# A hybrid decoder layer: three changes of order in the MLP's Strassen-like rounds, and a weight sum moved from GpSimd to VectorE

## The chip, the cores and the metric

The kernel runs on one core of a Trainium2 chip. The metric is the device time of one execution in microseconds (us), as the median of a few runs.

## What is computed

One decoder layer (DEPTH = 1) on 256 tokens of width 2048, everything in float32:

```
h = RMSNorm(x);  [b, c, xt, v] = h @ w_in            (2048 x 4096)
y_conv = b * causal_depthwise_conv3(c * xt)
y_pool = scale * per_group_linear(trailing_mean_w(v) - v)
x = x + concat(y_conv, y_pool) @ w_out               (2048 x 2048)
x = x + relu(RMSNorm(x) @ w_up)^2 @ w_down           (2048 x 8192, 8192 x 2048)
out = RMSNorm(x)
```

## The kernel before

**Precision.** TensorE multiplies in a reduced float32 format, so every operand is kept as a "hi" part and a "lo" part: ScalarE writes hi = round(raw), VectorE writes lo = raw - hi. A product is hi by hi, lo by hi and hi by lo. A weight is loaded into w_raw, split into w_hi (ScalarE, `hi_of`, L791) and w_lo (VectorE, `lo_of`, L1173), and used by TensorE. w_hi and w_lo have four slots each, used in turn, so hi of item g waits until TensorE has finished item g - 4 (`chunk_used`).

**Stages.** The projection w_in, the pool jobs, w_out, and then the MLP, which takes the span from about 290 us on. This case is about the MLP.

**The MLP.** w_up comes in 16 blocks t of 512 columns, each in four chunks of 1 MB. w_down is used in rounds d = t - 2: in round d (0 to 13) TensorE works on the four chunks of w_up block t = d + 2, and in between on w_down for blocks that are ready. Two blocks of hidden values with a half of w_down's columns form a 2 x 2 problem of quadrants that is done with seven products instead of eight. Each of the seven terms, one after another, is a product of a combination of value quadrants (S7, A11, N6, S5, A12, N3, A22) and a combination of weight quadrants (t3, b11, t2, t1, b21, t4, b22). An even and an odd round share the value combinations (slice s = d // 2).

**The order of TensorE in a round** (L587 to L608), written out by hand: up chunk 0, a11_b11, up chunk 1, n6_t2, a12_b21, up chunk 2, s7_t3 of round d + 1, s5_t1, up chunk 3, a22_t4, n3_b22. In round 0 s7_t3 of round 0 comes after up chunk 0. An up chunk is 16 hi matmuls (L557; the profile shows them at the helper's L395) and 16 lo matmuls (L398); a term is 8 matmuls with w_hi (L577, L579) and 4 with w_lo (L583). The same order of items (`item_order`, L38) numbers the weights for hi and lo.

**Folds.** Four terms go into bank NT of PSUM one after another, and VectorE adds or subtracts the bank into x after each (`fold`, L1203), with factors that make the accumulated sums come out right; a22_t4 goes on in the bank of s7_t3. TensorE waits for a fold before it writes on: a11_b11 for the fold of n3_b22 of round d - 1, n6_t2 for that of a11_b11, s5_t1 for that of n6_t2, n3_b22 for that of s5_t1. The folds count up one semaphore, and `fold_count` gives the count of each.

**Values.** When up chunk 3 of block t - 1 is done, ScalarE copies one half of the banks (`take_up`, L805), VectorE adds the other half and applies ReLU and the token's 1/rms (`add_up`, L1183, L1187), ScalarE squares (L810), VectorE makes the combinations ("parts", L1213, L1236, L1238, L1250), and both split them (`quad_hi` L816, `quad_lo` L1192).

**The weight sums of round d.** `sums[d % 2]` is loaded by SP with quadrant 1; GpSimd adds quadrant 3 by an accumulating DMA: that is t3 (`make_t3`, L371). After lo of s7_t3, and when quadrant 0 has landed in w_raw slot 2, the sum of both is t2 (L377 to L380): in the kernel before, a GpSimd addition over 128 x 2048. After lo of a11_b11 GpSimd adds quadrant 1 to slot 2 by DMA (t1), and after lo of n6_t2 it adds quadrant 2 to the sums (t4).

**VectorE's order in a round** (L1224 to L1279): fold s5_t1 (d - 1), lo up 0, add_up, lo a11_b11, parts, fold a22_t4 (d - 1), lo up 1, fold n3_b22 (d - 1), quad_lo's, lo n6_t2, quad_lo, lo a12_b21, fold a11_b11, quad_lo's, lo up 2, lo s7_t3 (d + 1), fold n6_t2, lo s5_t1, fold a12_b21, lo up 3, lo a22_t4, fold s7_t3 (d + 1), lo n3_b22. In even rounds there are two parts before the folds and one after, with two quad_lo's (L1192) more; in odd rounds one part before. In round 0 lo of s7_t3 stands after add_up.

After round 13 come eight plain products of w_down (`plain`, L621), the last of which wait for the last folds, and the final norm.

Of the kernel before, what the change touches and what calls it, by code (L numbers as in the profile page):

```python
# [15 lines left out]
NT = 4  # L16
# [7 lines left out]
FIRST_UP = FIRST_OUT + OUT_BLOCKS  # L24
UPS = D_FF // BLOCK_COLS
LEAD = 2
SEVENS = UPS - LEAD
# [25 lines left out]
ITEM = {name: FIRST_ITEM + i for i, name in enumerate(item_order())}  # L53
# [26 lines left out]
def build(nc, x_t, x_rows, w_stream, w_quads, pool_w, params, g_final, out):  # L80
# [4 lines left out]
    with ctx:  # L85
# [142 lines left out]
        def fold_count(d, term):  # L228

            if term == "s7_t3":  # L230
                return 1 if d == 0 else fold_count(d - 1, "a12_b21") + 1
            ahead = 1 if d + 1 < SEVENS else 0
            return 1 + 7 * d + {"a11_b11": 1, "n6_t2": 2, "a12_b21": 3, "s5_t1": 4 + ahead,
                                "a22_t4": 5 + ahead, "n3_b22": 6 + ahead}[term]

        def up_values(t):

# [7 lines left out]
        def bank_b(d):  # L245
            return NT + 1 + d % 2
# [112 lines left out]
        @block.gpsimd  # L359
        def _(pool):  # L360
            pool.memset(ones[:, :], 1.0).then_inc(consts_set, 1)
            pool.memset(win[:, :, :, 0:PAD], 0.0).then_inc(consts_set, 1)
            pool.wait_ge(x_lo_ready, KT)
            pool.memset(v[:, :, 0:PAD], 0.0).then_inc(v_pads_zero, 1)
            pool.wait_ge(pool_w_ready, 1)
            pool.memset(u[:, :, 0:2], 0.0).then_inc(u_pads_zero, 1)

            def add_quad(to, d, n, added):
                pool.dma_start(to, w_quads[4 * d + n, :, :], accum_op=ALU.add).then_inc(added, 16)  # L369

            def make_t3(d):  # L371
                pool.wait_ge(sum_base_loaded[d % 2], 16 * (d // 2 + 1))
                add_quad(sums[d % 2], d, 3, t3_added[d % 2])

            make_t3(0)
            for d in range(SEVENS):
                pool.wait_ge(lo_ready, ITEM["s7_t3", d] + 1)  # L377
                pool.wait_ge(raw_loaded[2], 16 * (FIRST_UP + LEAD + d + 1))
                pool.tensor_tensor(out=sums[d % 2], in0=sums[d % 2], in1=w_raw[:, 2, :], op=ALU.add)\  # L379
                    .then_inc(t2_added, 1)  # L380
                if d + 1 < SEVENS:
                    make_t3(d + 1)
                pool.wait_ge(t2_added, d + 1)
                pool.wait_ge(lo_ready, ITEM["a11_b11", d] + 1)
                add_quad(w_raw[:, 2, :], d, 1, t1_added)
                pool.wait_ge(lo_ready, ITEM["n6_t2", d] + 1)
                add_quad(sums[d % 2], d, 2, t4_added)
            pool.wait_ge(lo_ready, ITEM["a22_t4", SEVENS - 2] + 1)
            pool.dma_start(g_row, g_final[0:1, :].to_broadcast([P, D])).then_inc(g_loaded, 16)
# [256 lines left out]
        def _(act):  # L646
# [141 lines left out]
            def hi_of(g, raw):  # L788

                act.wait_ge(chunk_used, g - 3)  # L790
                act.activation(w_hi[:, g % 4, :], raw, ACT.Copy).then_inc(hi_ready, 1)  # L791
# [6 lines left out]
            def take_up(t):  # L798

                act.wait_ge(chunk_used, ITEM["up", t, CHUNKS - 1] + 1)  # L800
                if t >= 3:
                    act.wait_ge(quad_ready, quad_count((t - 3) // 2, N3))
                act.wait_ge(summed, turn(FIRST_UP) + t)
                banks = bank_halves(1 if t == 1 else 0, 1)
                act.activation(cross[:, :, :], banks, ACT.Copy).then_inc(cross_ready, 1)  # L805
# [23 lines left out]
            for t in range(LEAD, UPS):  # L829
                d, s = t - LEAD, (t - LEAD) // 2  # L830
                folding = d % 2 == 0
                up_hi(t, 0)
                take_up(t - 1)
                if d == 0:
                    act.wait_ge(t3_added[0], 16)
                    hi_of(ITEM["s7_t3", 0], sums[0])
                act.wait_ge(raw_loaded[2], 16 * (FIRST_UP + LEAD + d + 1))
                hi_of(ITEM["a11_b11", d], w_raw[:, 2, :])
                square_up(t - 1)
                up_hi(t, 1)  # L840
                if folding:
                    act.wait_ge(part_ready, parts + 2)
                    quad_hi(s, N6, part_1, "n6_t2")
                    quad_hi(s, S5, part_0, "s5_t1")
                elif s + 1 < SLICES - 1:
                    act.wait_ge(part_ready, parts + 1)
                    quad_hi(s + 1, S7, part_2, "s7_t3")
                else:
                    act.wait_ge(squared, t)
                    quad_hi(s + 1, A21, held[:, :, P:S])  # L850
                act.wait_ge(t2_added, d + 1)
                hi_of(ITEM["n6_t2", d], sums[d % 2])
                if folding:
                    act.wait_ge(squared, t)
                    quad_hi(s, A12, val[:, :, 0:P], "a12_b21")
                act.wait_ge(raw_loaded[3], 16 * (FIRST_UP + LEAD + 2 * d + 1))
                hi_of(ITEM["a12_b21", d], w_raw[:, 3, :])
                if folding:
                    act.wait_ge(part_ready, parts + 3)
                    quad_hi(s, N3, part_1, "n3_b22")  # L860
                    quad_hi(s, A22, val[:, :, P:S], "a22_t4")
                else:
                    act.wait_ge(squared, t)
                    quad_hi(s + 1, A11, held[:, :, 0:P], "a11_b11")
                parts += 3 if folding else 1
                up_hi(t, 2)
                if d + 1 < SEVENS:
                    act.wait_ge(t3_added[(d + 1) % 2], 16 * ((d + 1) // 2 + 1))
                    hi_of(ITEM["s7_t3", d + 1], sums[(d + 1) % 2])
                act.wait_ge(t1_added, 16 * (d + 1))  # L870
                hi_of(ITEM["s5_t1", d], w_raw[:, 2, :])
                up_hi(t, 3)
                act.wait_ge(t4_added, 16 * (d + 1))
                hi_of(ITEM["a22_t4", d], sums[d % 2])
                act.wait_ge(raw_loaded[3], 16 * (FIRST_UP + LEAD + 2 * d + 2))
                hi_of(ITEM["n3_b22", d], w_raw[:, 3, :])
# [31 lines left out]
        def _(dve):  # L908
# [262 lines left out]
            def lo_of(g, raw):  # L1171
                dve.wait_ge(hi_ready, g + 1)
                dve.tensor_tensor(out=w_lo[:, g % 4, :], in0=raw, in1=w_hi[:, g % 4, :].bitcast(F32),  # L1173
                                  op=ALU.subtract).then_inc(lo_ready, 1)
# [4 lines left out]
            def add_up(t):  # L1179

                to = up_values(t)
                dve.wait_ge(cross_ready, IN_CROSSES + t + 1)
                dve.tensor_tensor(out=to[:, :, :], in0=bank_halves(1 if t == 1 else 0, 0),  # L1183
                                  in1=cross[:, :, :], op=ALU.add).then_inc(summed, 1)
                dve.wait_ge(summed, turn(FIRST_UP) + t + 1)
                dve.wait_ge(inv_rms_ready, 2)
                dve.scalar_tensor_tensor(out=to[:, :, :], in0=to[:, :, :], scalar=0.0, in1=by_token(),  # L1187
                                         op0=ALU.max, op1=ALU.mult).then_inc(value_ready, 1)
# [7 lines left out]
            def fold(term, d, bank, t, n, op):  # L1196

                dve.wait_ge(chunk_used, ITEM[term, d] + 1)
                count = fold_count(d, term)
                if count > 1:  # L1200
                    dve.wait_ge(folded, count - 1)
                to = x_quad(d, t, n)
                dve.tensor_tensor(out=to, in0=to, in1=ps[:, bank, :], op=op).then_inc(folded, 1)  # L1203
# [20 lines left out]
            for t in range(LEAD, UPS):  # L1224
# [2 lines left out]
                if d:  # L1227
                    fold("s5_t1", d - 1, NT, 1, 1, ALU.subtract)
                up_lo(t, 0)
                add_up(t - 1)  # L1230
                if d == 0:
                    lo_of(ITEM["s7_t3", 0], sums[0])
                lo_of(ITEM["a11_b11", d], w_raw[:, 2, :])
                dve.wait_ge(squared, t)
                if folding:
# [4 lines left out]
                elif s + 1 < SLICES - 1:  # L1240
                    make_s7()
                if d:
                    fold("a22_t4", d - 1, bank_b(d - 1), 1, 0, ALU.add)
                up_lo(t, 1)
                if d:
                    fold("n3_b22", d - 1, NT, 0, 1, ALU.subtract)
                if folding:
                    quad_lo(s, N6, part_1)
                    quad_lo(s, S5, part_0)
# [31 lines left out]
            def plain_lo(f):  # L1281
                lo_of(ITEM["plain", f], w_raw[:, plain_raw(f)[0], :])
# [8 lines left out]
            fold("s5_t1", SEVENS - 1, NT, 1, 1, ALU.subtract)  # L1291
            plain_lo(0)
            add_up(UPS - 1)
            plain_lo(1)
            fold("a22_t4", SEVENS - 1, bank_b(SEVENS - 1), 1, 0, ALU.add)
            dve.wait_ge(squared, UPS)
            quad_lo(last_slice, A12, val[:, :, 0:P])
            quad_lo(last_slice, A22, val[:, :, P:S])
# [86 lines left out]
```

## Time and profile before

| what | value |
|---|---|
| median of 3 runs | 990.32 us (989.34 to 990.75) |
| the profiled execution, its own time | 989.43 us |
| its span, first to last instruction | 987.6 us |
| mean granted TensorE clock | 0.994 of full speed |
| TensorE busy | 954.1 us (97%) |
| VectorE busy | 787.4 us (80%) |
| ScalarE busy | 526.7 us (53%) |
| GpSimd busy | 114.8 us (12%) |
| mean DMA rate | 241 GB/s |

Times in the rows are microseconds from the first instruction; where one row stands for several instructions (x16), its time is that from the start of the first to the end of the last. PE is TensorE's matmuls, PEld its weight loads, DVE is VectorE, ACT ScalarE, POOL GpSimd. In square brackets stands how long the engine was idle before the instruction and what ended that. The ends of matmuls are modelled, and they overlap: the start of the next one is the better mark.

### The profile page before, as it was taken

The page shows a single profiled execution, that of the slowest core. Times are in us where ns is not written, and L with a number is a line of the kernel's source. Part 1 is how long each engine was busy: PE and PEld are TensorE (multiplying, and loading weights), DVE is VectorE, ACT ScalarE, POOL GpSimd, SP SyncE. Part 2 cuts the span into 40 slices and gives each one's busy share as a digit, 9 for nine tenths or more (in the row PEclk, how much of TensorE's full clock was granted, in tenths as well). Part 3 has the DMA queues.
Part 4 walks back from the last instruction along what each step waited for, and adds up shares of the span by engine and source line. Part 5 has one row for each costly group of instructions (what it writes and reads, how often), then busy time and mean ns, then how long its engine had stood idle before and what let it go on. Part 6 is the DMA issues. An engine that isn't in the chain of part 4 may idle for free.

```text
span 987.6 us, 12019 instructions
## 1 busy us (share of the span) xinstructions
PE 954.1 (97%) x4920; PEld 817.1 (83%) x4920; DVE 787.4 (80%) x605; ACT 526.7 (53%) x420; POOL 114.8 (12%) x65
## 2 busy tenths in 40 slices
PE   8999999999999969999999999999999999999996
PEld 7888888888888858888888888888888888888885
DVE  6597677655554789798988979989998997998864
ACT  6644435444543456565665556556555655646642
POOL 0000000000000303202031220203212020220000
PEclk9999999999999989999999999999999999999999
DMA  9956552644558198897989889898798979878822
GB/s 341 388 192 235 177 206 105 230 177 171 188 196 291 57 295 248 303 250 261 305 263 284 257 259 275 255 329 236 261 263 276 299 241 322 226 247 223 314 101 86
DMA packets 35763, 237.85 MB, mean 241 GB/s; under 512 B 3968, under 2 KB 4224, under 8 KB 7808
## 3 DMA queue, kind: packets, MB, share of 16 engines
q1 hardware_dynamic: 29232, 190.85, 50.3%
q0 software_dynamic: 6192, 45.09, 23.6%
q10 hardware_dynamic: 288, 1.18, 0.3%
q8 instruction: 37, 0.61, 0.2%
q14 instruction: 14, 0.11, 0.0%
HBM read 235.01 MB, written 2.10 MB: 240 GB/s over the span
## 4 chain that ended last, share of the span: by engine, by line
PE 62%; issue 16%; DVE 13%; ACT 6%; DMA 2%; SPq 0%; ACTq 0%; DVEq 0%
PE ps L395 22%; PE ps L398 12%; PE ps L486 9%; ACT w_hi L791 5%; PE ps L577 5%; PE ps L621 4%; PE ps L579 4%; PE ps L583 4%; DVE w_lo L1173 3%; DVE x L1203 3%; DMA w_raw<-w_stream 2%; DVE cross L1236 1%; DVE win L1187 1%; DVE val L1187 1%; DVE val L1183 1%
## 5 line engine op out<-in xcount | busy, mean ns | idle before, releaser
L395 PE MATMUL ps<-act_a,w_hi 128*128 128x512 f32 x1472 | 349.7, 390 | 0.0
L1173 DVE TENSOR_TENSOR w_lo<-w_raw,w_hi 128x2048 fp32r<-128x2048 f32 x120 | 316.7, 2639 | 10.2 <-ACT w_hi L791 9.0
L395 PEld LDWEIGHTS ps<-act_a,w_hi 128*128 128x128 f32 x1472 | 274.2, 188 | 55.5
L791 ACT ACTIVATE w_hi<-w_raw 128x2048 fp32r<-128x2048 f32 x120 | 229.5, 1913 | 71.0 <-PE ps L583 48.9
L398 PEld LDWEIGHTS ps<-act_a,w_lo 128*128 128x128 f32 x1472 | 188.5, 191 | 8.8 <-DVE w_lo L1173 1.9
L398 PE MATMUL ps<-act_a,w_lo 128*128 128x256 f32 x1472 | 191.2, 283 | 1.4 <-DVE w_lo L1173 1.4
L577 PE MATMUL ps<-w_hi,act_b 128*128 128x512 f32 x392 | 155.6, 397 | 18.8 <-DVE x L1203 18.8
L912 DVE TENSOR_TENSOR w_lo<-w_raw,w_hi 128x2048 fp32r<-128x2048 f32 x52 | 118.5, 2290 | 68.4 <-ACT w_hi L654 67.7
L579 PE MATMUL ps<-w_hi,act_b 128*128 128x512 f32 x392 | 154.1, 393 | 0.0
L1173 DVE TENSOR_TENSOR w_lo<-mix_mem,w_hi 128x2048 fp32r<-128x2048 f32 x42 | 104.8, 2496 | 48.6 <-ACT w_hi L791 48.1
L654 ACT ACTIVATE w_hi<-w_raw 128x2048 fp32r<-128x2048 f32 x52 | 98.9, 1911 | 65.5 <-PE ps L398 39.0
L791 ACT ACTIVATE w_hi<-mix_mem 128x2048 fp32r<-128x2048 f32 x42 | 80.2, 1910 | 89.4 <-PE ps L398 87.4
L379 POOL TENSOR_TENSOR mix_mem<-mix_mem,w_raw 128x2048 f32<-128x2048 f32 x14 | 76.9, 5494 | 265.2 <-DMA w_raw<-w_quads 233.9
L583 PE MATMUL ps<-w_lo,act_b 128*128 128x512 f32 x392 | 104.9, 389 | 0.0
L577 PEld LDWEIGHTS ps<-w_hi,act_b 128*128 128x128 f32 x392 | 74.3, 189 | 35.4 <-DVE x L1203 21.6
L583 PEld LDWEIGHTS ps<-w_lo,act_b 128*128 128x128 f32 x392 | 73.6, 188 | 15.5
L579 PEld LDWEIGHTS ps<-w_hi,act_b 128*128 128x128 f32 x392 | 74.4, 190 | 14.1
L1203 DVE TENSOR_TENSOR x<-x,ps 128x512 f32<-128x512 f32 x98 | 66.7, 681 | 3.3 <-PE ps L583 2.7
L486 PE MATMUL ps<-w_hi,act_b 128*128 128x512 f32 x256 | 68.8, 390 | 0.0
L369 POOL DMA_DIRECT2D mix_mem<-w_quads x28 | 24.5, 874 | 368.5 <-DMA mix_mem<-w_quads 272.2
L486 PEld LDWEIGHTS ps<-w_hi,act_b 128*128 128x128 f32 x256 | 47.8, 188 | 9.7
L805 ACT ACTIVATE cross<-ps 128x1024 f32<-128x1024 f32 x16 | 16.4, 1025 | 56.4 <-PE ps L398 56.4
(103 smaller groups left out, 593.6 us busy)
## 6 DMA issues: line engine op xcount, KB each, us to landing
w_raw<-w_stream SPq DMA_DIRECT2D x108, 1024.0 KB, 6.6
w_raw<-w_quads SPq DMA_DIRECT2D x50, 1024.0 KB, 8.6
mix_mem<-w_quads POOLq DMA_DIRECT2D x28, 1024.0 KB, 10.1
mix_mem<-w_quads SPq DMA_DIRECT2D x14, 1024.0 KB, 4.7
w_raw<-w_quads POOLq DMA_DIRECT2D x14, 1024.0 KB, 10.8
w_raw<-w_stream SPq DMA_DIRECT2D x16, 256.0 KB, 7.6
x<-x_rows SPq DMA_DIRECT2D x2, 1024.0 KB, 17.5
mix_mem<-x_t SPq DMA_DIRECT2D x3, 512.0 KB, 7.9
```

The lines of the kernel that those rows point to most:

```text
L379: pool.tensor_tensor(out=sums[d % 2], in0=sums[d % 2], in1=w_raw[:, 2, :], op=ALU.add)\
L395: return pe.matmul(ps[:, bank, :], weights_hi, act, start=first, stop=False)
L398: return pe.matmul(ps[:, bank, 0:S], weights_lo, act[:, 0:S], start=False, stop=last)
L486: mm = pe.matmul(ps[:, NT * parity + t, :], a[:, at:at + P], cols, start=first and i == 0, stop=last and i == 2)
L577: pe.matmul(to, quads[:, quad, k, 0:P], weights_of(w_hi, g, k), start=first and k == 0, stop=False, skip_group_check=not first)
L579: pe.matmul(to, quads[:, quad, k, P:2 * P], weights_of(w_hi, g, k), start=False, stop=False, skip_group_check=not first)
L583: mm = pe.matmul(to, quads[:, quad, k, 0:P], weights_of(w_lo, g, k), start=False, stop=k == CK - 1, skip_group_check=not first)
L654: act.activation(w_hi[:, c, :], w_raw[:, c, :], ACT.Copy).then_inc(hi_ready, 1)
L791: act.activation(w_hi[:, g % 4, :], raw, ACT.Copy).then_inc(hi_ready, 1)
L912: dve.tensor_tensor(out=w_lo[:, c, :], in0=w_raw[:, c, :], in1=w_hi[:, c, :].bitcast(F32), op=ALU.subtract)\
L1173: dve.tensor_tensor(out=w_lo[:, g % 4, :], in0=raw, in1=w_hi[:, g % 4, :].bitcast(F32), op=ALU.subtract).then_inc(lo_ready, 1)
L1203: dve.tensor_tensor(out=to, in0=to, in1=ps[:, bank, :], op=op).then_inc(folded, 1)
```

## The change

Four things are changed:

- The sum t2 (L379) is made by VectorE, between add_up and lo of a11_b11, with the same waits. GpSimd keeps only its DMAs.
- In a round, VectorE folds n3_b22 (d - 1) before lo up 1 and a22_t4 (d - 1) after it; before, it was the other way round. `fold_count` follows.
- In round 0, hi and lo of s7_t3 come before take_up and add_up instead of after them.
- After the last round, the fold of a22_t4 comes before the lo of plain product 1 instead of after it.

```diff
--- before.py
+++ after.py
@@ -229,9 +229,11 @@
 
             if term == "s7_t3":
                 return 1 if d == 0 else fold_count(d - 1, "a12_b21") + 1
-            ahead = 1 if d + 1 < SEVENS else 0
-            return 1 + 7 * d + {"a11_b11": 1, "n6_t2": 2, "a12_b21": 3, "s5_t1": 4 + ahead,
-                                "a22_t4": 5 + ahead, "n3_b22": 6 + ahead}[term]
+            if d + 1 < SEVENS:
+                ends = {"s5_t1": 5, "n3_b22": 6, "a22_t4": 7}
+            else:
+                ends = {"s5_t1": 4, "a22_t4": 5, "n3_b22": 6}
+            return 1 + 7 * d + ({"a11_b11": 1, "n6_t2": 2, "a12_b21": 3} | ends)[term]
 
         def up_values(t):
 
@@ -374,13 +376,8 @@
 
             make_t3(0)
             for d in range(SEVENS):
-                pool.wait_ge(lo_ready, ITEM["s7_t3", d] + 1)
-                pool.wait_ge(raw_loaded[2], 16 * (FIRST_UP + LEAD + d + 1))
-                pool.tensor_tensor(out=sums[d % 2], in0=sums[d % 2], in1=w_raw[:, 2, :], op=ALU.add)\
-                    .then_inc(t2_added, 1)
                 if d + 1 < SEVENS:
                     make_t3(d + 1)
-                pool.wait_ge(t2_added, d + 1)
                 pool.wait_ge(lo_ready, ITEM["a11_b11", d] + 1)
                 add_quad(w_raw[:, 2, :], d, 1, t1_added)
                 pool.wait_ge(lo_ready, ITEM["n6_t2", d] + 1)
@@ -830,10 +827,10 @@
                 d, s = t - LEAD, (t - LEAD) // 2
                 folding = d % 2 == 0
                 up_hi(t, 0)
-                take_up(t - 1)
                 if d == 0:
                     act.wait_ge(t3_added[0], 16)
                     hi_of(ITEM["s7_t3", 0], sums[0])
+                take_up(t - 1)
                 act.wait_ge(raw_loaded[2], 16 * (FIRST_UP + LEAD + d + 1))
                 hi_of(ITEM["a11_b11", d], w_raw[:, 2, :])
                 square_up(t - 1)
@@ -1227,9 +1224,13 @@
                 if d:
                     fold("s5_t1", d - 1, NT, 1, 1, ALU.subtract)
                 up_lo(t, 0)
-                add_up(t - 1)
                 if d == 0:
                     lo_of(ITEM["s7_t3", 0], sums[0])
+                add_up(t - 1)
+                dve.wait_ge(lo_ready, ITEM["s7_t3", d] + 1)
+                dve.wait_ge(raw_loaded[2], 16 * (FIRST_UP + LEAD + d + 1))
+                dve.tensor_tensor(out=sums[d % 2], in0=sums[d % 2], in1=w_raw[:, 2, :], op=ALU.add)\
+                   .then_inc(t2_added, 1)
                 lo_of(ITEM["a11_b11", d], w_raw[:, 2, :])
                 dve.wait_ge(squared, t)
                 if folding:
@@ -1240,10 +1241,10 @@
                 elif s + 1 < SLICES - 1:
                     make_s7()
                 if d:
-                    fold("a22_t4", d - 1, bank_b(d - 1), 1, 0, ALU.add)
+                    fold("n3_b22", d - 1, NT, 0, 1, ALU.subtract)
                 up_lo(t, 1)
                 if d:
-                    fold("n3_b22", d - 1, NT, 0, 1, ALU.subtract)
+                    fold("a22_t4", d - 1, bank_b(d - 1), 1, 0, ALU.add)
                 if folding:
                     quad_lo(s, N6, part_1)
                     quad_lo(s, S5, part_0)
@@ -1291,8 +1292,8 @@
             fold("s5_t1", SEVENS - 1, NT, 1, 1, ALU.subtract)
             plain_lo(0)
             add_up(UPS - 1)
+            fold("a22_t4", SEVENS - 1, bank_b(SEVENS - 1), 1, 0, ALU.add)
             plain_lo(1)
-            fold("a22_t4", SEVENS - 1, bank_b(SEVENS - 1), 1, 0, ALU.add)
             dve.wait_ge(squared, UPS)
             quad_lo(last_slice, A12, val[:, :, 0:P])
             quad_lo(last_slice, A22, val[:, :, P:S])
```

## Rows read from the trace of the kernel before

**Rows 1.** The page's engines: busy us (share of the span) and instructions.
```profile
PE 954.1 (97%) x4920; PEld 817.1 (83%) x4920; DVE 787.4 (80%) x605; ACT 526.7 (53%) x420; POOL 114.8 (12%) x65
```
**Rows 2.** Waits: engine, line, releaser: us in total, times, longest us.
```profile
PE ps L577 <- DVE x L1203: 18.8, 14, 6.5
```
**Rows 3.** TensorE's timeline, an odd and an even round: start us, us, instruction.
```profile
557.96 2.07 PE L398 MATMUL ps<-act_a,w_lo 128*128 128x256 f32 x16
560.57 0.50 PE L577 MATMUL ps<-w_hi,act_b 128*128 128x512 f32 x1 [0.54 <-DVE x L1203]
...
563.43 3.79 PE L395 MATMUL ps<-act_a,w_hi 128*128 128x512 f32 x16
...
568.97 0.40 PE L577 MATMUL ps<-w_hi,act_b 128*128 128x512 f32 x1
...
571.72 0.39 PE L577 MATMUL ps<-w_hi,act_b 128*128 128x512 f32 x1
...
603.41 0.50 PE L577 MATMUL ps<-w_hi,act_b 128*128 128x512 f32 x1 [1.26 <-DVE x L1203]
...
611.82 0.40 PE L577 MATMUL ps<-w_hi,act_b 128*128 128x512 f32 x1
```
**Rows 4.** The page's groups: busy us, mean ns of one | idle before, releaser.
```profile
L791 ACT ACTIVATE w_hi<-mix_mem 128x2048 fp32r<-128x2048 f32 x42 | 80.2, 1910 | 89.4 <-PE ps L398 87.4
L379 POOL TENSOR_TENSOR mix_mem<-mix_mem,w_raw 128x2048 f32<-128x2048 f32 x14 | 76.9, 5494 | 265.2 <-DMA w_raw<-w_quads 233.9
```
**Rows 5.** VectorE's timeline, from the odd round into the even one.
```profile
565.56 0.68 DVE L1203 TENSOR_TENSOR x<-x,ps 128x512 f32<-128x512 f32 x1
...
585.00 6.11 DVE L1173 TENSOR_TENSOR w_lo<-w_raw,w_hi 128x2048 fp32r<-128x2048 f32 x1
...
593.83 1.21 DVE L1183 TENSOR_TENSOR val<-ps,cross 128x1024 f32<-128x1024 f32 x1
...
596.22 2.28 DVE L1173 TENSOR_TENSOR w_lo<-w_raw,w_hi 128x2048 fp32r<-128x2048 f32 x1
598.42 0.68 DVE L1236 TENSOR_TENSOR cross<-val,win 128x512 f32<-128x512 f32 x1
...
599.87 0.69 DVE L1203 TENSOR_TENSOR x<-x,ps 128x512 f32<-128x512 f32 x1
...
610.59 0.68 DVE L1203 TENSOR_TENSOR x<-x,ps 128x512 f32<-128x512 f32 x1
```
**Rows 6.** The timeline of all engines around 590 us: GpSimd's sum and ScalarE's copy.
```profile
583.29 5.66 POOL L379 TENSOR_TENSOR mix_mem<-mix_mem,w_raw 128x2048 f32<-128x2048 f32 x1 [18.70 <-DMA w_raw<-w_quads]
...
591.19 1.03 ACT L805 ACTIVATE cross<-ps 128x1024 f32<-128x1024 f32 x1 [3.56 <-PE ps L398]
```
**Rows 7.** The page's DMA issues: count, KB each, median us to landing.
```profile
w_raw<-w_quads POOLq DMA_DIRECT2D x14, 1024.0 KB, 10.8
```
**Rows 8.** Timelines of ScalarE, VectorE and TensorE in the first round.
```profile
330.57 1.03 ACT L805 ACTIVATE cross<-ps 128x1024 f32<-128x1024 f32 x1 [6.52 <-PE ps L398]
...
338.43 5.10 DVE L1236 TENSOR_TENSOR cross<-val,win 128x512 f32<-128x512 f32 x1
...
353.81 1.47 DVE L1203 TENSOR_TENSOR x<-x,ps 128x512 f32<-128x512 f32 x2
...
355.33 0.80 PE L577 MATMUL ps<-w_hi,act_b 128*128 128x512 f32 x1 [6.52 <-DVE x L1203]
...
362.36 3.79 PE L395 MATMUL ps<-act_a,w_hi 128*128 128x512 f32 x16
```
**Rows 9.** A window: us, busy us of each engine, TensorE clock, DMA share, GB/s.
```profile
352.00:353.00 1.00, 0.00 (x0) 0.00 (x0) 1.00 (x1) 1.00 (x2) 0.11 (x1) 0.50 1.04 246
```
**Rows 10.** Timelines of VectorE and TensorE at the start of the plain products.
```profile
932.76 2.29 DVE L1173 TENSOR_TENSOR w_lo<-w_raw,w_hi 128x2048 fp32r<-128x2048 f32 x1
934.96 0.68 DVE L1203 TENSOR_TENSOR x<-x,ps 128x512 f32<-128x512 f32 x1
...
935.75 1.17 PE L621 MATMUL ps<-w_hi,act_b 128*128 128x512 f32 x4 [1.02 <-issue]
```

## The prediction, made before the change was run

> **What bounds the kernel now.** I read the page's table of engines first: TensorE is busy 97% of the span [rows 1]. So only time in which TensorE stands still can be won. The table of waits shows where that is: matmuls of L577, the first product of a term of w_down, waited 14 times for the fold at L1203, 18.8 us in all [rows 2]. The timeline of TensorE sorts these 14. One, in the first round (d = 0), is 6.52 us [rows 8]. The other 13 add to 12.28 us and recur with the parity of d, always before a11_b11, which needs the fold of n3_b22 of the round before: 1.26 us in the six even rounds (603.41 stands for them), 0.54 us in five of the seven odd ones (560.57), 4.72 us in the seven together [rows 3]. A last gap of 1.02 us stands before the plain products [rows 10].
>
> A stall costs more than its idle time. A w_up chunk without one takes 568.97 - 563.43 = 5.54 us, and the lo half that ends it started at 557.96; the next start without a stall comes 1.91 us after it (my reading of the same rows: the 16 lo products step by 0.12), so at 559.87, and it came at 560.57: 0.70. The term then took 563.43 - 560.57 = 2.86 us against 571.72 - 568.97 = 2.75 [rows 3]. So each stall costs its idle time plus 0.27 us: 1.53 us in an even round.
>
> Next, who is late. VectorE runs the even round without a gap from 585.00 on [rows 5]. One instruction there, a w_lo subtraction, took 6.11 us where its neighbours step by 2.20 us (596.22 to 598.42). GpSimd's sum ran from 583.29 to 588.95, over its start [rows 6]. Such a long VectorE instruction stands beside each of the 14 sums; in the first round it is the 5.10 us at 338.43, where its kind takes 0.68 us elsewhere [rows 5, 8]. The sum itself has a mean of 5.49 us on GpSimd [rows 4].
>
> **The change part by part.**
>
> *The sum leaves GpSimd.* The long instruction falls from 6.11 to 2.28 us, 3.83 us less. VectorE would then be free for add_up at 593.83 - 3.83 = 590.00, but ScalarE's copy of the cross half starts at 591.19, when TensorE has ended the chunk, and takes 1.03 us [rows 6]. So add_up starts at 592.25, not 593.83: only 1.58 us of the 3.83 is of use, 2.25 us is slack.
>
> *The sum goes to VectorE.* No row has an f32 addition of 128x2048 there. From below it is bounded by the subtraction of the same size, which also reads two SBUF operands and steps by 2.20 us [rows 5]; from above by the sum on GpSimd, 5.49 us [rows 4]. I take 2.20, since engine, shape and operand kinds are those of the subtraction. At 5.49 the first and the six even rounds would lose 3.3 us each and the seven odd ones about 2.1, together 38 us; no VectorE row is near that, so the range leaves it out. The Trainium skill (GPSIMD Engine Reference, Key points) says that VectorE is structurally about twice as fast for elementwise work: by that factor 5.49 us would become 2.75, and the time would be 3.8 us longer than forecast below (seven chains by 0.55). The subtraction's row, 2.4 times faster than the GpSimd sum, goes before it.
> The sum stands between add_up and the lo of a11_b11. Its new waits end long before: its w_raw slot had landed when GpSimd's sum began at 583.29, 11 us earlier. Queued behind it are the lo of a11_b11, the two parts, both folds, the lo of a12_b21 and the fold of a11_b11. All of them come -1.58 + 2.20 = 0.62 us later than now.
>
> *n3_b22 is folded ahead of a22_t4 and of a w_up lo.* It takes the place at 599.87 [rows 5]: start 600.49, end 601.17. TensorE wants it when the chunk ends, at 603.41 - 1.42 = 601.99. The stall before a11_b11 is gone in the even rounds; in the odd ones, with one part less to make, there is more room still.
> What is late next is the fold of a11_b11, for which n6_t2 waits. Even round: it starts at 610.59 now [rows 5], so at 611.21, and ends at 611.89. TensorE would be there at 611.82 - 1.53 = 610.29 [rows 3]. New stall: n6_t2 starts at 611.95, 1.66 us late, 1.77 with the slow start. Six even rounds: 6 x (1.53 - 1.77) = **-1.4 us**, a loss. Odd round: the fold starts at 565.56 + 0.62 and ends at 566.9, and TensorE wants it at 568.97 - 0.81 = 568.16 [rows 3, 5]. No stall, so the whole 4.72 + 7 x 0.27 = **+6.6 us** is won.
> The later fold of a22_t4 costs nothing: TensorE's next use of its bank is s7_t3, a whole w_up chunk after n6_t2, which waits for more. If that cover were gone, the price would be the 2.8 us that it moves.
>
> *First round.* The s7_t3 pair moves ahead of take_up and add_up. ScalarE idles 6.52 us before that take_up [rows 8], which covers the pair: a hi of 1.91 us [rows 4] and, behind it, the lo of 2.2 us. Its t3 is made by the first DMA that GpSimd issues in this stage. The lo of s7_t3 thus leaves the chain and the sum enters it, 2.20 against 2.20. The instruction at 338.43 loses 5.10 - 0.68 = 4.42 us. Every instruction from there to the pair of folds at 353.81 follows without a gap, so they end at 350.9 and n6_t2 starts there instead of at 355.33: **+4.4 us**. TensorE has stood still since 355.33 - 6.52 = 348.8 in the trace; its wait for a w_up lo in the chunk before, whose lo comes 4.4 us sooner too, goes as well, so it will stand from about 347, and a gap of 4 us stays.
> The clock: in that standstill it fell to half (1.2 of 2.4 GHz), as granted at 352 to 353 [rows 9]; the two terms after it took 362.36 - 355.33 = 7.03 us instead of 2.86 + 2.75 = 5.61 [rows 8]. With the shorter gap this 1.4 us may be lost as before or won whole. Between a standstill of 6.5 us that loses the clock and stalls of 1.3 us that keep it there is no row for 4 us; I take the middle, **+0.7 us**, and keep 0 and 1.4 for the range.
>
> *Tail.* The fold of a22_t4 moves ahead of plain_lo(1), to 932.76, and ends at 933.44 instead of 935.64. TensorE's last term ends about 934.7, so the gap of 1.02 us goes, with the slow start **+1.2 us** [rows 10]. plain_lo(1) comes 0.6 us later, at 935.6 done; its product starts 5.4 us after the first, at about 940.
>
> *GpSimd's queue.* Its three accumulating DMAs a round stay. t3 no longer stands behind the sum, so it is issued up to 0.5 us sooner, in the first round much sooner. t1 and t4 follow the lo of a11_b11 and n6_t2, so they come 0.6 us later. They land in 10.8 us [rows 7], and their readers on TensorE, s5_t1 and a22_t4, stand two chunks and three or four terms on, at least 2 x 5.54 + 3 x 2.75 = 19 us. SP's loads wait for the same lo's and shift by as little. Cost nothing; without that slack 0.6 us a round.
>
> Sum: 4.4 + 0.7 + 6.6 - 1.4 + 1.2 = 11.5 us. The profiled execution took 989.43 us (span 987.6), which gives 977.9; the median of the runs, 990.32, is 0.9 above it, so I forecast **978.8 us**.
>
> **The rivals.**
> 1. *The long VectorE instruction has another cause than the sum* (the DMAs around it, say). Then the 3.83 us stays and 2.20 us is added. Against the forecast the first round loses 4.4 + 0.7, the six even rounds 6 x 1.58 = 9.5, and the odd ones get a stall of 568.50 - 568.16 and a slow start, 0.45 x 7 = 3.2: 17.8 us, so 978.8 + 17.8 = 996.6, **slower than before**. It decides from about 3.5 us of the 3.83 staying. Against it: all 14 coincide, also where the sum lay over another instruction. The Trainium skill (SBUF — State Buffer, SBUF: two separate sides) says that a VectorE instruction with two SBUF inputs and a GpSimd one that reads SBUF exclude each other for the whole instruction; by that rule the long instruction goes with the sum, and the trace agrees: 588.95 - 585.00 = 3.95 us of overlap, 3.83 us longer. Chance 0.04.
> 2. *The sum costs more on VectorE than the subtraction*, by 0.5 to 1 us (two waits ahead of it, in-place output). Each 0.1 us costs 0.7 us (six even chains and the first); at +0.5 it gives 982.3. The odd rounds stay out up to +1.2. Every two-input SBUF row of VectorE speaks against it. Chance 0.10.
> 3. *The first round's gain does not come*: DMA is busy in full there, and an earlier round may meet loads that have not landed. Then 978.8 + 5.1 = 983.9. For it: a DMA share of 1.04 at 352 to 353 [rows 9]. Against: no wait for a load there now, and t3's transfer leaves that stretch. Chance 0.10.
> 4. *The n6_t2 stall is smaller* because something in the chain has slack I don't see; without it 978.8 - 6 x 1.77 = 968. Against: VectorE's rows have no gap in that chain. Chance 0.06.
>
> **How the numbers follow.** Forecast with its bounds (clock 0.7 either way, spread of runs 0.7): 977 to 980.5, chance 0.70. The range reaches to rivals 2 and 3 above and partly towards 4: 975 to 984. A measurement of this kernel can tell about 0.2% (2 us). Faster by more than that: forecast and rivals 2 to 4, 0.95. Slower: rival 1 nearly, 0.03. Within: 0.02, the edge of rival 1 where part of the slowdown stays.
>
> **What would show it.** No GpSimd TENSOR_TENSOR and no VectorE instruction over 2.4 us among the w_lo ones; 14 new ones of 2.28 us. In the waits, L577 waits for L1203 seven times instead of 14: about 4 us at d = 0, and about 1.5 us before n6_t2 at each even d; none in odd rounds. A pair of rounds gets 0.81 - 0.24 = 0.6 us shorter. No gap before the plain products. Stalls before a11_b11 that stay, or waits of ScalarE for a DMA, would make it wrong.

## The result, and the profile after

The changed kernel takes **979.29 us** (median of 4 runs, 978.88 to 979.58), the kernel before 990.54 beside it: ratio 0.9885 (95% interval 0.9868 to 0.9902), 11.3 us faster. 978.8 was forecast.

The span went from 987.6 to 977.8 us. The page of the changed kernel, its engines and the groups that answer to [rows 1, 4]; in the changed kernel the subtraction is L1170 (was L1173), the sum L1232, the fold L1200 (was L1203):

```profile
PE 951.9 (97%) x4920; PEld 816.8 (84%) x4920; DVE 763.8 (78%) x619; ACT 527.0 (54%) x420; POOL 37.8 (4%) x51
...
L1170 DVE TENSOR_TENSOR w_lo<-w_raw,w_hi 128x2048 fp32r<-128x2048 f32 x120 | 274.3, 2286 | 9.2 <-ACT w_hi L788 8.2
```

And from its table of groups for VectorE:

```profile
L1232 DVE TENSOR_TENSOR mix_mem<-mix_mem,w_raw 128x2048 f32<-128x2048 f32 x14 | 32.0, 2285 | 0.0
```

VectorE has 14 instructions more and is busy 23.6 us less: the 14 sums add 32.0 us, and what GpSimd's sums had stretched is gone (the w_lo subtractions of L1170 have means of 2286 and, from the sums, 2291 ns, and the longest takes 2.30 us). The waits of TensorE for a fold, which answer to [rows 2]:

```profile
PE ps L574 <- DVE x L1200: 12.9, 7, 3.8
```

Seven instead of 14. TensorE's timeline shows which (columns as in [rows 3]): the one of round 0, and the even rounds, all before n6_t2; 606.45 stands for six of 1.50 to 1.51 us.

```profile
350.82 0.80 PE L574 MATMUL ps<-w_hi,act_b 128*128 128x512 f32 x1 [3.81 <-DVE x L1200]
...
602.87 2.07 PE L395 MATMUL ps<-act_a,w_lo 128*128 128x256 f32 x16
606.45 0.50 PE L574 MATMUL ps<-w_hi,act_b 128*128 128x512 f32 x1 [1.51 <-DVE x L1200]
```

VectorE's timeline of that even round, from add_up to the fold of a11_b11 (answers to [rows 5]), with ScalarE's copy ahead of it from the timeline of ScalarE:

```profile
585.69 1.03 ACT L802 ACTIVATE cross<-ps 128x1024 f32<-128x1024 f32 x1 [3.56 <-PE ps L395]
```

```profile
586.75 1.23 DVE L1180 TENSOR_TENSOR val<-ps,cross 128x1024 f32<-128x1024 f32 x1 [2.17 <-ACT cross L802]
...
589.15 2.29 DVE L1232 TENSOR_TENSOR mix_mem<-mix_mem,w_raw 128x2048 f32<-128x2048 f32 x1
591.35 2.28 DVE L1170 TENSOR_TENSOR w_lo<-w_raw,w_hi 128x2048 fp32r<-128x2048 f32 x1
...
605.71 0.68 DVE L1200 TENSOR_TENSOR x<-x,ps 128x512 f32<-128x512 f32 x1
```

VectorE now waits 2.17 us for ScalarE's copy before add_up (2.25 were reckoned); the sum steps by 2.20 us; the fold of a11_b11 ends at 606.39, and TensorE goes on at 606.45. From the copy's start to the end of this fold it is 606.39 - 585.69 = 20.70 us now and was 611.27 - 591.19 = 20.08 [rows 5, 6]: the chain is the 0.62 us longer that were worked out. To n6_t2 it is 20.76 us now and was 20.63 [rows 3, 6], because TensorE, held up before a11_b11, came after that fold then and waits for it now.

Round 0 and the clock, in windows of the changed kernel (columns as in [rows 9]):

```profile
348.00:349.00 1.00, 0.00 (x0) 0.00 (x0) 1.00 (x1) 1.00 (x1) 0.00 (x0) 1.00 1.34 279
349.00:350.00 1.00, 0.00 (x0) 0.00 (x0) 0.97 (x2) 0.69 (x1) 0.00 (x0) 0.66 0.70 123
...
354.00:355.00 1.00, 1.00 (x4) 0.81 (x3) 1.00 (x2) 0.00 (x0) 0.00 (x0) 0.50 0.90 344
```

The granted clock fell to half in the 3.8 us standstill too, and in this execution it came back later than before: in TensorE's timeline the chunk after the two terms starts at 358.85, so they took 358.85 - 350.82 = 8.03 us, against 7.03 [rows 8]. That 1.0 us is not the length of the standstill. Two of the runs below that keep this part of the changed kernel have the same standstill, and there the two terms took 7.13 and 6.94 us (this is the run with the fold order undone):

```profile
351.31 0.80 PE L572 MATMUL ps<-w_hi,act_b 128*128 128x512 f32 x1 [3.83 <-DVE x L1198]
...
358.25 3.79 PE L390 MATMUL ps<-act_a,w_hi 128*128 128x512 f32 x16
```

And after a standstill of 6.52 us, as before the change, they took 8.16 us in the run with the folds alone. So the clock's cost varies between 1.3 and 2.6 us over the 5.6 us of the full clock, after the short and after the long standstill alike.

The tail: VectorE folds at 924.05, TensorE goes from its last term to the plain products without a gap ([rows 10] had one of 1.02 us).

```profile
924.05 0.68 DVE L1200 TENSOR_TENSOR x<-x,ps 128x512 f32<-128x512 f32 x1
```

```profile
924.96 1.07 PE L580 MATMUL ps<-w_lo,act_b 128*128 128x512 f32 x4
925.86 1.07 PE L618 MATMUL ps<-w_hi,act_b 128*128 128x512 f32 x4
```

### The profile page after: what moved, and what is told of

Its sections match the earlier page's. It is cut to its first block, busy times and chain, and to the rows that moved or that the text cites. A ratio compares the mean times of both kernels' runs of the same rounds, so it can differ in the third digit from the quotient of the medians.

```text
span 977.8 us, 12003 instructions
## 1 busy us (share of the span) xinstructions
PE 951.9 (97%) x4920; PEld 816.8 (84%) x4920; DVE 763.8 (78%) x619; ACT 527.0 (54%) x420; POOL 37.8 (4%) x51
## 4 chain that ended last, share of the span: by engine, by line
PE 79%; DVE 10%; issue 5%; DMA 2%; ACT 2%; SPq 1%; ACTq 0%; DVEq 0%
PE ps L392 28%; PE ps L395 15%; PE ps L483 9%; PE ps L574 8%; PE ps L576 7%; PE ps L580 7%; PE ps L618 4%; DMA w_raw<-w_stream 2%; DVE w_lo L1170 2%; DVE mix_mem L1232 2%; DVE act_b L1189 1%; DVE x L1200 1%; DVE val L1180 1%; ACT cross L802 1%; DVE cross L1239 1%
## 5 line engine op out<-in xcount | busy, mean ns | idle before, releaser
L1170 DVE TENSOR_TENSOR w_lo<-w_raw,w_hi 128x2048 fp32r<-128x2048 f32 x120 | 274.3, 2286 | 9.2 <-ACT w_hi L788 8.2
L909 DVE TENSOR_TENSOR w_lo<-w_raw,w_hi 128x2048 fp32r<-128x2048 f32 x52 | 118.5, 2291 | 67.3 <-ACT w_hi L651 66.6
L1170 DVE TENSOR_TENSOR w_lo<-mix_mem,w_hi 128x2048 fp32r<-128x2048 f32 x42 | 96.2, 2291 | 38.2 <-ACT w_hi L788 37.7
L580 PE MATMUL ps<-w_lo,act_b 128*128 128x512 f32 x392 | 105.6, 391 | 0.0
L580 PEld LDWEIGHTS ps<-w_lo,act_b 128*128 128x128 f32 x392 | 74.2, 189 | 15.6
L1200 DVE TENSOR_TENSOR x<-x,ps 128x512 f32<-128x512 f32 x98 | 66.8, 681 | 2.6 <-PE ps L580 2.0
L483 PE MATMUL ps<-w_lo,act_b 128*128 128x512 f32 x128 | 39.4, 389 | 0.0
## 6 DMA issues: line engine op xcount, KB each, us to landing
mix_mem<-w_quads POOLq DMA_DIRECT2D x28, 1024.0 KB, 10.8
x<-x_rows SPq DMA_DIRECT2D x2, 1024.0 KB, 16.2
```

Source lines behind the costliest of these rows:

```text
L483: mm = pe.matmul(ps[:, NT * parity + t, :], a[:, at:at + P], cols, start=first and i == 0, stop=last and i == 2)
L580: mm = pe.matmul(to, quads[:, quad, k, 0:P], weights_of(w_lo, g, k), start=False, stop=k == CK - 1, skip_group_check=not first)
L909: dve.tensor_tensor(out=w_lo[:, c, :], in0=w_raw[:, c, :], in1=w_hi[:, c, :].bitcast(F32), op=ALU.subtract)\
```

## The experiments

The theory, called C: TensorE is let go by VectorE's folds, so only what moves along the chain from ScalarE's copy to the fold that TensorE needs counts. Its rival, called G: GpSimd's sum, which held VectorE up for 3.83 us a round, was the loss, and the orders are trimmings. The sum of the parts came out right, but the prediction had never said which part won, the move or the orders. All medians are set beside 990.3 to 990.9 us for the kernel before and 979.3 us for the changed one.

**The move of the sum alone** (the kernel before, with this):

```diff
-                pool.wait_ge(lo_ready, ITEM["s7_t3", d] + 1)
-                pool.wait_ge(raw_loaded[2], 16 * (FIRST_UP + LEAD + d + 1))
-                pool.tensor_tensor(out=sums[d % 2], in0=sums[d % 2], in1=w_raw[:, 2, :], op=ALU.add)\
-                    .then_inc(t2_added, 1)
...
-                pool.wait_ge(t2_added, d + 1)
...
+                dve.wait_ge(lo_ready, ITEM["s7_t3", d] + 1)
+                dve.wait_ge(raw_loaded[2], 16 * (FIRST_UP + LEAD + d + 1))
+                dve.tensor_tensor(out=sums[d % 2], in0=sums[d % 2], in1=w_raw[:, 2, :], op=ALU.add)\
+                   .then_inc(t2_added, 1)
                 lo_of(ITEM["a11_b11", d], w_raw[:, 2, :])
```

> The sum on VectorE, every order as before. Theory C (the chain: what counts is when VectorE's folds let TensorE go on): in a steady round VectorE reaches add_up 1.58 us sooner but carries 2.20 us more, so n3_b22 is folded 0.62 us later and both kinds of stall before a11_b11 grow: 13 x 0.62 = +8.1 us; the first round wins 4.42 - 2.20 = 2.2. In all 990.5 + 5.9, about 996 us, slower than before. Theory G (GpSimd's sum was the loss, the orders are trimmings): most of the 11 us gain is here, 980 to 984 us.

Measured: 999.29 us (ratio to before 1.0098, 1.0078 to 1.0118), **9 us slower than before**. G falls: the change's headline, alone, makes the kernel slower. The even stalls before a11_b11 have grown by 0.63 us each, and four of the seven odd ones by 0.62, as C has it (timeline of TensorE; 1.26 and 0.54 in [rows 3]):

```profile
518.23 0.50 PE L572 MATMUL ps<-w_hi,act_b 128*128 128x512 f32 x1 [1.89 <-DVE x L1198]
...
562.60 0.50 PE L572 MATMUL ps<-w_hi,act_b 128*128 128x512 f32 x1 [1.16 <-DVE x L1198]
```

C's figure is 3 us short. The windows of this run show why: behind the stall of 1.89 us the clock fell to half for about 3 us.

```profile
518.20:519.00 0.80, 0.77 (x3) 0.67 (x4) 0.77 (x2) 0.80 (x1) 0.00 (x0) 1.00 1.03 215
519.00:519.50 0.50, 0.50 (x4) 0.38 (x3) 0.50 (x1) 0.50 (x1) 0.00 (x0) 1.00 1.02 213
519.50:520.00 0.50, 0.50 (x3) 0.40 (x2) 0.47 (x2) 0.46 (x1) 0.00 (x0) 0.59 1.10 229
...
522.50:523.00 0.50, 0.50 (x3) 0.41 (x2) 0.50 (x2) 0.32 (x1) 0.15 (x1) 0.50 1.04 442
523.00:524.00 1.00, 1.00 (x6) 0.83 (x5) 0.97 (x2) 1.00 (x1) 0.72 (x1) 1.00 0.32 131
```

From this round's a11_b11 to the next one's is 562.60 - 518.23 = 44.37 us, where a pair with the clock kept takes 42.75 (432.00 to 474.75): 1.6 us. It happened in three of the six even rounds, 4.9 us. That is more than the missing 3 us, because the other three odd stalls hardly grew: the seven went from 4.72 to 7.39 us together, 1.7 us less than C has it.

**The folds alone** (the kernel before; VectorE's order and `fold_count` as in the change):

```diff
                 if d:
-                    fold("a22_t4", d - 1, bank_b(d - 1), 1, 0, ALU.add)
+                    fold("n3_b22", d - 1, NT, 0, 1, ALU.subtract)
                 up_lo(t, 1)
                 if d:
-                    fold("n3_b22", d - 1, NT, 0, 1, ALU.subtract)
+                    fold("a22_t4", d - 1, bank_b(d - 1), 1, 0, ALU.add)
```

> Only the folds of n3_b22 and a22_t4 change places; the sum stays on GpSimd, round 0 and the tail stay. Theory C: the stall before a11_b11 goes in all 13 rounds (the seven odd ones win 6.6 us); in the six even ones n6_t2 waits instead, 1.15 us against 1.53: +2.3. About 8.9 us faster than before, 981.6 us. Theory G: little, 988 to 990.5 us.

Measured: 981.93 us (0.9912, 0.9895 to 0.9928), as C has it. No stall in odd rounds; six of 0.88 us before n6_t2.

**All of the orders without the move** (the changed kernel, with the first diff of this section backwards):

> The changed kernel with the sum back on GpSimd (all of the orders, not the move). Theory C: the stall before n6_t2 in the six even rounds is 0.62 us shorter than with the sum on VectorE, 3.7 us in all; round 0 is the same within 1 us, because GpSimd's sum now begins while VectorE still waits for ScalarE's copy. About 975.5 us (974.5 to 977), faster than the changed kernel. Theory G: the gain is mostly lost, 985 to 989 us.

Measured: 971.87 us (0.9812, 0.9795 to 0.9828), **7.4 us faster than the changed kernel**. The even stall is 0.88 us instead of 1.51, six times 0.63. In round 0 the gap is 1.96 us instead of 3.81, and the clock stayed full behind it, which C's figure had left out and which puts the result below its range: 1.9 us of gap and 1.3 to 2.4 of clock. So the long instruction of round 0 goes by the order alone, and the sum on VectorE takes 1.9 us of that back. The timeline of TensorE in this run:

```profile
351.55 0.50 PE L579 MATMUL ps<-w_hi,act_b 128*128 128x512 f32 x1 [1.96 <-DVE x L1205]
435.33 0.50 PE L579 MATMUL ps<-w_hi,act_b 128*128 128x512 f32 x1 [0.88 <-DVE x L1205]
```

**The fold order undone** (the changed kernel, the diff of the second experiment backwards):

> The changed kernel with the folds of n3_b22 and a22_t4 in their old places (the sum on VectorE, round 0 and tail as changed). Theory C: all 13 rounds stall before a11_b11 as in the run with the sum alone, 2.15 us in the even rounds and 1.43 in the odd ones, against 1.77 and 0: +2.3 and +10.0 us, and the stalls near 1.9 us cost the clock in about half of the even rounds, 1.6 us each: 979.3 + 12.3 + 4.8 = 996 us (992 if the clock holds). Theory G: 981 us or less.

Measured: 994.93 us (1.0044, 1.0026 to 1.0062). With the sum on VectorE this one exchange is worth 15.6 us; even stalls are 1.89 us, odd ones 1.16, and the clock fell behind three of the six.

**GpSimd's sum and the VectorE instruction at once** (the changed kernel; VectorE's instruction leaves the values as they are):

```diff
+                pool.wait_ge(lo_ready, ITEM["s7_t3", d] + 1)
+                pool.wait_ge(raw_loaded[2], 16 * (FIRST_UP + LEAD + d + 1))
+                pool.tensor_tensor(out=sums[d % 2], in0=sums[d % 2], in1=w_raw[:, 2, :], op=ALU.add)\
+                    .then_inc(t2_by_pool, 1)
...
-                dve.tensor_tensor(out=sums[d % 2], in0=sums[d % 2], in1=w_raw[:, 2, :], op=ALU.add)\
+                dve.wait_ge(t2_by_pool, d + 1)
+                dve.tensor_tensor(out=sums[d % 2], in0=sums[d % 2], in1=sums[d % 2], op=ALU.max)\
```

> The changed kernel, but GpSimd makes the sum where it did before, and VectorE an instruction of the same size in place of its sum (a maximum with itself). Both costs at once, the price of rival 1 of the prediction. If GpSimd's sum is what holds VectorE up: 14 long VectorE instructions are back, 1.58 us of each is on the chain, even rounds lose 6 x 1.58, odd ones 7 x 0.45, round 0 up to 1.5: 979.3 + 13.5 = about 993 us. If something else held it up in the kernel before, no long instruction comes back and the time is 979 to 980 us.

Measured: 994.81 us (1.0044, 1.0031 to 1.0057). The long instruction is back with GpSimd's sum in 13 of the 14 rounds (in round 0 the sum lies over add_up, see the last section), in one round as 6.12 us from 586.32, beside GpSimd's 5.57 us from 584.73 (timelines of VectorE and GpSimd):

```profile
586.32 6.12 DVE L1175 TENSOR_TENSOR w_lo<-w_raw,w_hi 128x2048 fp32r<-128x2048 f32 x1
```

```profile
584.73 5.57 POOL L382 TENSOR_TENSOR mix_mem<-mix_mem,w_raw 128x2048 f32<-128x2048 f32 x1 [16.25 <-DMA w_raw<-w_quads]
```

So the sum on GpSimd is the cause of the long instruction, which was only argued before, and another cause, as rival 1 has it, is out. The price of having both, 15.5 us, is near the 17.8 of rival 1 and the 13.5 above, but in part by luck, since the places are others: even rounds stall twice, 0.66 to 1.00 us before a11_b11 and 2.1 us before n6_t2, and odd rounds not at all. The clock fell in three of the six, 4.8 us, which more than makes up for the 3.2 us of the odd rounds.

**A longer chain** (the changed kernel, one more VectorE instruction behind the sum; values stay):

```diff
+                dve.wait_ge(t2_once, d + 1)
+                half_sum = sums[d % 2][:, 0:CHUNK_W // 2]
+                dve.tensor_tensor(out=half_sum, in0=half_sum, in1=half_sum, op=ALU.max)\
+                   .then_inc(t2_added, 1)
```

> The changed kernel with a second VectorE instruction right behind the sum, over half its columns (the maximum of each element with itself, so values stay), about 1.15 us and a wait of 0.1 us. Theory C with the chain as worked out: each of the six even rounds and round 0 lose all of it, 7 x 1.25 = 8.8 us, the odd rounds nothing, because their fold of a11_b11 is 1.26 us early: 988 us. If VectorE's sum were a matter of its load and not of the chain, all 14 rounds would lose alike (17.5 us, 997 us), or none (979 us) while it has idle time.

Measured: 990.88 us (1.0005, 0.9995 to 1.0015), no faster than the kernel before. Odd rounds lose nothing, even ones 0.35 us before a11_b11 and 0.65 more before n6_t2, and a slow start each:

```profile
515.50 0.50 PE L575 MATMUL ps<-w_hi,act_b 128*128 128x512 f32 x1 [0.35 <-DVE x L1201]
526.20 0.50 PE L575 MATMUL ps<-w_hi,act_b 128*128 128x512 f32 x1 [2.15 <-DVE x L1201]
```

So the chain has the length that was worked out. The 2.8 us over C's figure are again the clock, lost behind two of the six stalls of 2.15 us.

**Round 0 and the tail, each undone** (the changed kernel with the order of before at the one place):

```diff
                 up_hi(t, 0)
+                take_up(t - 1)
                 if d == 0:
                     act.wait_ge(t3_added[0], 16)
                     hi_of(ITEM["s7_t3", 0], sums[0])
-                take_up(t - 1)
...
-                if d == 0:
-                    lo_of(ITEM["s7_t3", 0], sums[0])
                 add_up(t - 1)
+                if d == 0:
+                    lo_of(ITEM["s7_t3", 0], sums[0])
```

> The changed kernel with the s7_t3 pair of round 0 behind take_up and add_up again. Theory C: the lo stands in the chain, n6_t2 of round 0 starts 2.2 us later, and the clock is lost either way: 981.5 us. Rival: the pair had cover there too, 979.3 us.

Measured: 981.33 us (0.9902, 0.9887 to 0.9918), 2.0 more. n6_t2 of round 0 starts at 353.00 instead of 350.82.

```diff
-            fold("a22_t4", SEVENS - 1, bank_b(SEVENS - 1), 1, 0, ALU.add)
             plain_lo(1)
+            fold("a22_t4", SEVENS - 1, bank_b(SEVENS - 1), 1, 0, ALU.add)
```

> The changed kernel with the last fold of a22_t4 behind plain_lo(1) again. Theory C: the gap of 1.02 us before the plain products is back with its slow start, 979.3 + 1.2 = 980.5 us. Rival: the products behind it have slack and give it back by the end, 979.3 us.

Measured: 980.55 us (0.9900, 0.9883 to 0.9917), 1.3 more, and the gap of 1.02 us is back. Both differences are near what the runs can tell; the timelines carry them.

**The next stall taken away** (the changed kernel):

```diff
                 lo_of(ITEM["n6_t2", d], sums[d % 2])
-                if folding:
-                    quad_lo(s, A12, val[:, :, 0:P])
-                lo_of(ITEM["a12_b21", d], w_raw[:, 3, :])
                 if d == 0:
                     fold("s7_t3", 0, bank_b(0), 1, 1, ALU.subtract)
                 fold("a11_b11", d, NT, 0, 0, ALU.add)
+                if folding:
+                    quad_lo(s, A12, val[:, :, 0:P])
+                lo_of(ITEM["a12_b21", d], w_raw[:, 3, :])
```

> The changed kernel, and in each round the fold of a11_b11 stands ahead of the lo of a12_b21 (in round 0 that of s7_t3 with it), 2.2 to 2.9 us sooner. Theory C: no stall before n6_t2 in even rounds, 6 x 1.77 = 10.6 us; in round 0 2.9 us less, and TensorE then stands for 1 us only, so the clock is kept and 2.4 us more are won: 963.4 us (965.8 if the clock falls all the same). Rival D (VectorE as a whole is the bound of an even round, so the wait only moves on to the next fold, before s5_t1): half or less of the 10.6 us, 969 us or more.

Measured: **963.09 us** (0.9725, 0.9708 to 0.9741), 16.2 us below the changed kernel. One stall is left in the whole of the rounds, and from 352 to 940 us TensorE is busy without a gap (window: us, then PE, PEld, DVE, ACT, POOL busy, clock, DMA share, GB/s):

```profile
347.77 0.50 PE L574 MATMUL ps<-w_hi,act_b 128*128 128x512 f32 x1 [0.90 <-DVE x L1200]
```

```profile
352.00:940.00 588.00, 588.00 (x2998) 503.71 (x2996) 517.17 (x365) 346.12 (x236) 33.44 (x39) 1.00 0.89 271
```

VectorE, 88% busy there, was never the bound as a whole: rival D falls.

**The same with the sum on GpSimd** (both edits together):

> The kernel with the fold of a11_b11 ahead of the lo of a12_b21, and the sum on GpSimd again. Theory C: with that fold early nothing waits for VectorE in a steady round, so where the sum is made does not matter: 962 to 963.5 us, as with the sum on VectorE (963.1), perhaps 0.9 us less in round 0. If the move of the sum is worth something by itself it shows here, 966 us or more.

Measured: **961.86 us** (0.9705, 0.9692 to 0.9718), the fastest here. In this run GpSimd still holds VectorE up in every round but the first, and it costs nothing (groups of VectorE; 2286 ns in the changed kernel):

```profile
L1175 DVE TENSOR_TENSOR w_lo<-w_raw,w_hi 128x2048 fp32r<-128x2048 f32 x120 | 323.9, 2699 | 8.9 <-ACT w_hi L793 7.7
```

The 1.2 us that it is faster than the run before are near what the runs can tell; the 0.90 us of idle time and the slow start of round 0, which are gone, are of that size.

## Why the prediction was right, step by step

- *The long instruction goes with the sum, of 3.83 us only 1.58 of use.* Right: add_up waits 2.17 us for ScalarE, and the run with both instructions shows the cause.
- *2.20 us on VectorE.* Right: 2.285 us each, steps of 2.20. The factor of two of the Trainium skill (GPSIMD Engine Reference, Key points) would have given 2.75; the measurement decides for the subtraction's row.
- *Odd rounds +6.6 us.* Right: no stall in any.
- *Even rounds -1.4 us.* Right: six of 1.51 us idle before n6_t2, where 1.66 less the 0.16 of modelled overlap were forecast.
- *Round 0 +4.4 us.* Right in size: n6_t2 at 350.82 instead of 355.33. But the orders alone give more, counted from the start of a11_b11: 13.12 us to n6_t2, against 14.98 in the changed kernel and 19.40 before.
- *The clock +0.7 us.* Wrong, the one mis-sized term: a standstill of 3.8 us lost the clock as one of 6.5 did. In the two profiled executions the term is **-1.0** (8.03 against 7.03 us), but over the kept traces the two terms took 8.03, 7.13 and 6.94 us after 3.8 us and 7.03 and 8.16 after 6.5, so what the change does to it is about 0, and the rest is chance. The range for this term, 0 to 1.4, should have reached below zero, as it left out that this loss varies from one execution to the next.
- *Tail +1.2 us.* Right: 1.3 by its undoing.
- *Sum.* The terms give 11.5; the profiled executions differ by 989.43 - 979.58 = 9.85. The 1.7 us between are the clock's term in these two. With 0 for it the terms give 10.8, near the 11.3 by which the median fell. Part of the closeness of 978.8 to 979.29 is luck all the same: the median before lies 1.1 us above its profiled run, the median after 0.3 below.
- *Rivals.* 1: the sum was the cause, so its condition was not met; its price was about right. 2 and 3 did not come. 4 neither: the stall before n6_t2 is there in full.

What the prediction left unsaid stands in its own numbers: -1.58 + 2.20 is a loss of 0.62 us a round. The move costs, and the orders win:

| the sum on | order before | orders of the change | and the fold of a11_b11 early |
|---|---|---|---|
| GpSimd | 990.3 | 971.9 | 961.9 |
| VectorE | 999.3 | 979.3 | 963.1 |

## What to carry to other kernels

An instruction that another engine stretches costs only what the stretch puts on the chain after its slack; read what stands behind it (here a wait for ScalarE of 2.25 us) before paying 2.2 us to remove 3.8. When several edits come together, price each of them by itself: the headline edit can be the one that loses. Where one engine's order sets another free, put what the other waits for ahead of what it needs only later: moving one fold past one or two subtractions was worth 16 us here, twice, with the sum on VectorE (with it on GpSimd the first of the two was worth 8.4, the second 10.0).

## What was not expected of the hardware

- **Short stalls can cost the clock.** Of the even-round stalls of 1.5 us in the changed kernel none was followed by a fall; of those of 1.89 us in two kernels 6 of 12 were, of 2.1 to 2.16 us in two others 5 of 12, each for about 3 us at half clock (1.6 us lost). In the first kernel with 1.89 us the fall came after TensorE had started again (519.50, restart 518.23). So a stall of 1.9 us costs up to 3.5 and its slow start, and what 0.6 us more on the chain costs is not linear. Length alone does not decide it, since stalls of the same 1.89 or 2.15 us went both ways. Of the single gaps in round 0, 1.96 us kept the clock and 3.81 us did not. What else decides was not tried.
- **GpSimd's sum does not stop every VectorE instruction, and the two stop each other.** In the kernel before, a fold, which reads PSUM and one tile of SBUF, lay wholly under GpSimd's sum of [rows 6] and took its usual time (timeline of VectorE):

```profile
582.19 2.29 DVE L1173 TENSOR_TENSOR w_lo<-mix_mem,w_hi 128x2048 fp32r<-128x2048 f32 x1 [3.11 <-ACT w_hi L791]
584.40 0.68 DVE L1203 TENSOR_TENSOR x<-x,ps 128x512 f32<-128x512 f32 x1
```

So did one in 10 of the 14 rounds. The subtraction behind it, the one of 6.11 us in [rows 5], ended 591.11 - 588.95 = 2.16 us after the sum, about its own length: it got nowhere while the sum ran. The other way round, the sum took 4.61 us at the least, and 5.66 where VectorE's subtraction before that fold, from 582.19, lay over its first 1.19 us.

  With the orders alone, GpSimd's sum of round 0 lay over add_up. The first instruction, which reads PSUM and one tile of SBUF, took its usual 1.23 us under it; the second, which reads two tiles of SBUF, took 1.56 instead of 1.23 and ended 1.1 us after GpSimd did (timeline of all engines):

```profile
331.23 4.63 POOL L381 TENSOR_TENSOR mix_mem<-mix_mem,w_raw 128x2048 f32<-128x2048 f32 x1 [23.53 <-DVE w_lo L1175]
...
334.12 1.23 DVE L1185 TENSOR_TENSOR val<-ps,cross 128x1024 f32<-128x1024 f32 x1 [2.98 <-ACT cross L807]
335.38 1.56 DVE L1189 SCALAR_TENSOR_TENSOR val<-val,inv_rms 128x1024 f32<-128x1024 f32 x1
```

The Trainium skill (SBUF — State Buffer, SBUF: two separate sides) names just this: two SBUF inputs of VectorE against a GpSimd instruction that reads SBUF. The traces agree, with 0.68 us for the folds, 1.23 for add_up and 6.11 for the subtraction. By that rule the place of GpSimd's sum could be chosen over instructions that read PSUM; a kernel laid out for it was not run.
